# A chunk's two decays next to each other on ScalarE, and the query-score products moved up on VectorE

## The reference

```
decay = exp(where(incl, gc[..., :, None] - gc[..., None, :], -inf))
m     = where(strict, (k_beta @ k.T) * decay, 0)      # inverted: (I + m)^-1
intra = (q @ k.T) * decay                             # used for the outputs
```

## Time and profile before

| | |
|---|---|
| median of 3 runs | 1077.85 us (1075.97 to 1080.37) |
| the profiled execution | 1074.18 us, span 1072.4 us |
| mean granted TensorE clock | 0.935 of full |
| TensorE matmul busy | 907.4 us (85%) |
| VectorE busy | 652.2 us (61%) |
| ScalarE busy | 518.0 us (48%) |
| GpSimd busy | 187.0 us (17%) |

### The profile page before, as it was taken

How to read it: one execution, slowest core, us unless ns; L and a number is a source line. 1 busy time by engine, 2 the same in 40 slices (tenths; PEclk the granted TensorE clock), 3 DMA queues, 4 the chain that set the end, 5 groups by cost and what they waited for, 6 DMA issues and landing times. The chain is left out here.

```text
span 1072.4 us, 14130 instructions
## 1 busy us (share of the span) xinstructions
PE 907.4 (85%) x5500; PEld 768.4 (72%) x5500; DVE 652.2 (61%) x840; ACT 518.0 (48%) x827; POOL 187.0 (17%) x323
## 2 busy tenths in 40 slices
PE   3999888988889888898676998794799999999982
PEld 0578777887778777788675878774587877777761
DVE  1277455444665446644364544656888888888874
ACT  2365542325433354332562214434477777777761
POOL 3103050012500125001241000003212111111103
PEclk9899988999899998999987999895999999999996
DMA  8555546433474334743447342770689999999973
GB/s 302 178 174 152 131 100 198 123 94 92 95 222 119 94 99 89 215 124 94 165 127 212 120 129 93 252 273 2 217 315 368 389 388 378 381 374 385 382 303 138
DMA packets 218893, 216.79 MB, mean 202 GB/s; under 512 B 33168, under 2 KB 154681, under 8 KB 218185
## 3 DMA queue, kind: packets, MB, share of 16 engines
q1 hardware_dynamic: 216089, 205.90, 59.3%
q0 software_dynamic: 2736, 9.96, 2.4%
HBM read 194.83 MB, written 21.00 MB: 201 GB/s over the span
## 5 line engine op out<-in xcount | busy, mean ns | idle before, releaser
L1911 DVE TENSOR_TENSOR w_lo<-raw,w_hi 128x2048 fp32r<-128x2048 f32 x96 | 224.8, 2351 | 48.0 <-ACT w_hi L1383 47.4
L2114 PE MATMUL bank<-hT,half_hi 128*128 128x256 f32 (+1 forms) x1024 | 238.2, 329 | 16.1 <-ACT staged L1079 12.6
L1383 ACT CAST w_hi<-raw 128x2048 fp32r<-128x2048 f32 x96 | 183.3, 1911 | 79.7 <-DMA raw<-in_w_e_dram 68.1
L2114 PEld LDWEIGHTS bank<-hT,half_hi 128*128 128x128 f32 x1024 | 175.8, 201 | 33.2 <-ACT staged L1079 13.6
L1509 DVE TENSOR_TENSOR half_lo<-half_raw,half_hi 128x1024 fp32r<-128x1024 f32 x88 | 108.9, 1239 | 108.2 <-ACT half_hi L981 107.8
L2114 PE MATMUL bank<-hT,half_lo 128*128 128x256 f32 (+1 forms) x512 | 164.7, 322 | 0.0
L2114 PE MATMUL bank<-lane 128*128 128x128 f32 (+1 forms) x1072 | 140.9, 292 | 24.6 <-DMA lane<-inverse 13.3
L2114 PEld LDWEIGHTS bank<-lane 128*128 128x128 f32 (+1 forms) x1072 | 130.1, 199 | 35.5 <-issue 19.4
L2114 PE MATMUL bank<-w_hi,window 128*128 128x512 f32 x480 | 155.3, 399 | 0.0
L2114 PEld LDWEIGHTS bank<-hT,half_lo 128*128 128x128 f32 x512 | 102.7, 201 | 6.1
L981 ACT CAST half_hi<-half_raw 128x1024 fp32r<-128x1024 f32 x88 | 92.3, 1052 | 30.0 <-PE bank L2114 15.8
(11 more groups left out here) (302 smaller groups left out, 1312.5 us busy)
## 6 DMA issues: line engine op xcount, KB each, us to landing
raw<-in_w_e_dram SPq DMA_DIRECT2D x96, 1024.0 KB, 7.8
half_raw<-in_w_in_dram SPq DMA_DIRECT2D x64, 512.0 KB, 4.2
half_raw<-in_w_ada_dram SPq DMA_DIRECT2D x32, 512.0 KB, 4.2
raw<-in_w_ada_dram SPq DMA_DIRECT2D x8, 1024.0 KB, 9.8
expert_rows<-y_out POOLq DMA_DIRECT2D x15, 512.0 KB, 7.4
dense<-staged SPq DMA_DIRECT2D x32, 128.0 KB, 2.8
lane<-inverse SPq DMA_DIRECT2D x16, 256.0 KB, 5.5
lane<-inverse_turned SPq DMA_DIRECT2D x16, 256.0 KB, 5.3
```

The source lines that it names most:

```text
L1383: act.copy(e_hi[n % WBUF][:, :], raw[n % RING][:, :]).then_inc(s["hi_ready"], 1)
L1911: dve.tensor_tensor(e_lo[n % WBUF][:, :], raw[n % RING][:, :], e_hi[n % WBUF][:, :].bitcast(F32), ALU.subtract)\
L2114: return nc.tensor.matmul(dst, lhsT, rhs, start=start, stop=stop)
```

## The change

In the loop over pairs 0 to 2, ScalarE makes `intra_exp(2)` right behind `decay_exp(2)`, ahead of the rounding of a weight half and of `decay_exp(3)`, and `intra_exp(3)` right behind `decay_exp(3)`. Both stood later, `intra_exp(2)` between the output scaling of the pair before and `dense_copy`, `intra_exp(3)` between `center(1)` and `squares(0, 0)`. VectorE makes `intra_mask(2)` right behind `first_level(3)`, ahead of the low part of a weight half and of `taps(0)`; it stood between `taps(0)` and `silu(0)`. `intra_mask(3)` stays. No instruction and no wait is added or removed, TensorE's, SP's and GpSimd's orders are as they were, and pair 3 keeps its order.

```diff
@@ ScalarE, loop over pairs 0 to 2
                 ahead(CHAN_AT[j, 0])
                 decay_exp(1)
                 decay_exp(2)
+                intra_exp(2)
                 ahead(CHAN_AT[j, 1])
                 decay_exp(3)
+                intra_exp(3)
                 ahead(DENSE_AT[3 + 7 * i + 0])
                 center(0)
                 if i:
                     o_mul(i - 1)
-                intra_exp(2)
                 dense_copy(3 + 7 * i + 0)
                 tanh(0)
                 center(1)
-                intra_exp(3)
                 squares(0, 0)
                 ahead(DENSE_AT[3 + 7 * i + 1])
                 tanh(1)
@@ VectorE, loop over pairs 0 to 2
                 ahead(CHAN_AT[j, 1])
                 first_level(2)
                 first_level(3)
+                intra_mask(2)
                 ahead(DENSE_AT[3 + 7 * i + 0])
                 taps(0)
-                intra_mask(2)
                 silu(0)
                 taps(1)
                 intra_mask(3)
```

## The result

The changed kernel takes 1082.47 us (median of 20 runs, 1080.16 the lowest), the kernel before, in the 20 runs beside it, 1077.19. The ratio is 1.005 with a 95% interval of 1.003 to 1.0071: half a per cent slower. One run of the changed kernel, at 1206.97 us and a granted clock of 0.732, counts in its median (1082.20 without it) and not in the ratio.

A forecast was written before the change was run, and what follows sets the result against it. Bound: TensorE's wait for the scaled keys, set by a chain of ScalarE, VectorE, SP, DMA and GpSimd running beside it. 3 pairs x 1.4 = +4.2 us on the median 1077.85 gave 1082.0 us; range 1077 to 1087.

The forecast's parts named there:

- (a): ScalarE: early `intra_exp(2)` takes 1.70 us, delays the weight half's rounding by that, and fits the 1.78 us gap before `decay_exp(3)`.
- (b): VectorE: the half's low part (L1509) delays `first_level(2)` and the third tile's `m_ready` 1.7 us, `first_level(3)` only 0.3.
- (c): SP and DMA: rows of tiles 0 to 2 leave 1.7 us late, tile 3's 0.3; blocks 1.4 late per pair.
- only the last row move counts: Rival at the row moves: blocks only 0.3 us late per pair, +1.0 us, 1078.9 us; chance 0.18.
- (d): VectorE, first silu: late taps (0.6 us) and bare tanh (0.7) offset the moved product; silu 0.1 late, not 1.3 early.
- (e): TensorE, pairs 1 and 2: `turn_out` no longer waits for `intra_exp(3)`, so `turn_channels(0)` starts 1.9 us sooner; pair 0 unchanged.
- (f): TensorE before `turn_back(0, 0)`: the 1.9 us gain is lost waiting for keys; stalls become 4.0, 5.2 and 5.9 us.
- The clock: TensorE after the longer stall for the keys: extra time at the lower clock priced at 0, bounds 0 to 0.3 per pair.
- One to one to the end of the pair: Premise for everything behind `turn_back(0, 0)`: fixed order, so a shift there passes undiminished to the pair's end.
- a sign of being wrong: Later part of the pair (inverse loads, 3.16 us stall in pair 0): prediction fails if it takes up the lateness.
- The slower rival: At the blocks: full 1.7 us arrives plus 0.2 from queueing with the weight half; 5.7 us, 1083.6 us; chance 0.27.
- The faster rival: TensorE's 1.9 us gain in two pairs reaches the end: -3.8 to -7.5 us, 1074.1 to 1070.4; chance 0.08.

The follow-up runs named there:

- The second: Kernel before with only `intra_exp(2)` moved to right behind `decay_exp(2)`, `intra_exp(3)` and both products left in place: 1081.68 us, ratio 1.0046.
- the first experiment: Changed kernel with `intra_exp(2)` one place later, behind the rounding of the weight half, still ahead of `decay_exp(3)`: 1077.65 us, ratio 1.0012.
- sixth experiment: Changed kernel with SP issuing the load of a 512 KB weight half behind `move_blocks` instead of ahead of it: 1081.94 us, ratio 1.0051.
- ninth experiment: On top of the first experiment, `first_level(2)` on VectorE and the first row move on SP go ahead of the weight half: 1078.32 us, ratio 0.9998.
- third: Changed kernel with GpSimd's `key_norm(0)` made inside the block solve, ahead of its sixth step: 1070.18 us, ratio 0.9937; run again, 1071.21 us, 0.9951.
- fourth: Kernel before with GpSimd's `key_norm(0)` made inside the block solve, ahead of its sixth step: 1073.75 us, ratio 0.9967.
- eighth: Changed kernel with `intra_exp(2)` split, its four Relus ahead of the rounding of the weight half, its Exp behind it: 1079.43 us, ratio 1.0039.

## Why the prediction came out right

The forecast was 1082.0 us, 4.2 above the median before, and the slower side of half a per cent at 0.28. Measured are 1082.47 and 1.005, on the bound itself. Some of the closeness is luck. The kernel before came out 0.66 lower over 20 runs than over the three that the forecast stood on, so the forecast of 4.2 us missed by 0.8 to 1.2: the distance is 5.0 to 5.4 us, near the upper edge of the forecast's own band (1.8 per pair, 5.4). And the range had a slip that did not matter: its lower bounds, 0.9 above the median less 3 for the scatter, give 1075.8 and not 1077. Step by step:

(a) *The rounding 1.7 late, the fourth decay spared.* Held: 13.7 against 12.0 us, and 14.9 against 14.8.

(b) *VectorE passes it on.* Held: L1509 1.7 late, `first_level(2)` behind it. The second and the first experiment show that this one position makes and removes the loss.

(c) *Of the 1.7, 1.4 arrive at the blocks.* The mechanism held, the term was too small and one part of it wrong. First rows to fetch of the blocks is 6.5, 6.3 and 6.2 us before and 6.4, 7.75 and 6.5 after, 6.2 in all pairs of the sixth experiment: at most 0.3 of the 1.7 is made up. I had the rows of tile 3 leave 0.3 late. They go in two issues, the third and fourth of the four. The third did begin 0.3 late, but took 1.62 us where it took 0.36 before, and so the fourth began 1.55 late: in pair 1 the four issues end at 264.34, 20.5 us into the pair, before at 264.35, 19.0 into it. The third issue in the queue's timelines in pair 1, of the changed kernel and of the kernel before:

```profile
261.99 1.62 SPq L511 DMA_DIRECT2D problem_rows<-lane  x1
...
263.21 0.36 SPq L511 DMA_DIRECT2D problem_rows<-lane  x1
```

How long it takes goes with how soon it follows the first two, the large ones of 384 KB: 0.6 us behind the second it takes 1.33 to 1.92 us, 1.0 behind it 1.23 to 1.33, and 2.0 or more behind it 0.36, over all pairs of all runs here. In the first two cases it ends 2.4 to 3.0 us after the first issue began, whichever pair one takes. So the last, small move hangs on the first, large ones, and the rival "only the last row move counts" failed in its first sentence, the blocks 0.3 late: in no pair of the changed kernel are they less than 1.6 late. What the Trainium skill gives ("DMA: Bandwidth & Descriptors", Anatomy of one DMA), a fixed 2 us plus bytes over 436 GB/s, pointed the same way as that rival; here the measurement decides, 3.3 us for 128 KB and 4.8 in the changed kernel, medians of two. Only with the ninth experiment's order, where the large moves went out 4 us ahead, do the 128 KB land in 2.1 to 2.5 us, about the 2.3 of that formula.

(d) *The first silu neither early nor late.* Held: 24.3 against 24.2 in pair 1; the taps went out late and the tanh stood bare, as the two sides of that sum had it.

(e) *`turn_channels(0)` 1.9 sooner in pairs 1 and 2, not in pair 0.* Held in every pair: 25.0 against 26.9, and 25.0 in pair 0.

(f) *Swallowed.* Held, and seen from three sides: the first experiment has the gain and no loss and lies at the kernel before (1.0012); the second has the loss and no gain and lies at the changed kernel (1.0046); the third and fourth free the keys, and the order of the two kernels turns round, in their medians though not beyond their intervals. The forecast of the stalls was 4.0, 5.2 and 5.9 us; they are 4.55, 6.31 and 5.58.

*The clock* was priced at 0, with up to 0.3 a pair. That bound was too small. In pair 1 of the changed kernel, after the 6.31 us stall and after a 4.70 us stall for the inverses, the rows are:

```profile
288.90:293.60 4.70, 4.64 (x13) 3.87 (x14) 3.56 (x5) 2.32 (x4) 0.53 (x1) 0.50 0.47 136
...
313.60:317.60 4.00, 4.00 (x21) 4.00 (x22) 1.38 (x2) 0.00 (x0) 0.00 (x0) 0.57 1.14 298
```

The first stretch is all at half clock (0.50), where the same stretch had 0.64 behind a stall of 1.93 us: 0.14 x 4.7, some 0.7 us more lost. The second is `level_p(0)`, which in the kernel before followed a stall of 1.73 us at full clock:

```profile
310.00:314.00 4.00, 4.00 (x36) 4.00 (x37) 3.04 (x6) 0.00 (x0) 0.00 (x0) 1.00 1.17 293
```

That is another 1.7 us (0.43 x 4.0) in this pair of this execution. Pair 1 lost 6.7 us in all: 2.7 up to `turn_back(0, 0)`, 2.4 from there to `level_p(0)` (24.6 us, 22.2 before; the wait for the inverses is 3.0 longer) and 1.6 from there to the next pair. It is not a steady price: pair 0 of the kernel before also waited over 3 us there, and its 32 products took 6.53 us, those of this pair 5.44.

*One to one to the end of the pair.* This premise is the weak step. In pair 0 the change came 1.67 us late to `turn_back(0, 0)`, 1.2 late to `level_p(0)` and 0.1 late to the next pair: the later part took the lateness up, which the prediction had named as a sign of being wrong. In pair 2 it was 1.4, 1.9 and 3.0. From `level_p(0)` to the next pair TensorE idles 5.12 to 5.14 us in 37 of the 39 pairs of all runs, and yet the stretch takes from 68.7 to 72.0 us: the rest is the granted clock, in the third column from the right (PEclk). Pair 0 before and after, then pair 1 before and after:

```profile
173.92:245.39 71.47, 64.67 (x508) 59.48 (x509) 33.31 (x60) 20.14 (x48) 6.20 (x10) 0.96 0.37 104
...
173.51:243.88 70.37, 63.58 (x508) 58.38 (x509) 33.35 (x61) 20.17 (x48) 6.22 (x10) 0.98 0.37 107
...
310.00:378.73 68.73, 61.93 (x509) 56.75 (x509) 34.09 (x62) 20.15 (x48) 6.21 (x10) 1.00 0.40 110
...
313.60:383.97 70.37, 63.57 (x508) 58.38 (x509) 33.29 (x60) 20.17 (x48) 6.21 (x10) 0.98 0.38 106
```

Behind a stall of at most 1.73 us for the inverses, or none, it is 68.7 to 69.6 us (8 pairs), behind a longer one 70.1 to 72.0 (30 of 31 pairs), and among these the longer stall is often not the dearer. So a shift reaches the pair's end only with such steps of 1 to 3 us on top, either way. That three of them add up to about the measured loss holds for the mean over many executions; no single trace shows it. With 1.6 in place of 1.4 in (c) the sum is 4.8; what the clock and the wait for the inverses add on the mean of many executions, one profile can't tell. Measured are 5.0 (medians, without the run at 1206.97) to 5.4 (ratio).

The slower rival had the right size (5.7) for a wrong reason: the load that shares the queue was taken from beside the rows in the sixth experiment and the time stayed. The faster rival fell with the first.

## What to carry to other kernels

A small group put into an engine's idle gap delays what is queued directly behind it, even when the next instruction that one watches, here the fourth decay, is untouched; follow the neighbour it was put in front of, through every engine that handles it in order, down to the DMA queue. When a stall is removed, look for the next point where the same engine waits for another chain: what was won in front of it shows only after that wait is gone. And lateness can cost in full where the same earliness shows nothing, as in the eighth and ninth experiments here, so one experiment in each direction tells more than two in the same.

## What the runs showed of the hardware

SP's issue of a transfer is not of fixed length. The third issue of a row move took 0.36 us when it followed the two large ones by 2.0 us or more, 1.23 to 1.33 when it followed by 1.0, and 1.33 to 1.92 when it followed by 0.6. The rate of the DMA engines does not decide it: the issue of 0.36 us fell where they moved 344 GB/s, and the one of 1.62 us where they moved 296 in the mean. A chain that counts issues as free will put one that follows large transfers closely too early.

A stall of TensorE can cost twice, as wait and as clock, but its length alone doesn't tell the second price. Over the 4 us behind it the granted clock had a mean of 0.50 to 0.65 after every stall of 4.0 us and more in the loop. After shorter ones it was either: 1.00 after 3.39 us in the eighth experiment's pair 0, 0.67 after 3.40 us in pair 2 of the kernel before. And after the same 1.67 us at the start of a pair it was 1.00 in 17 cases of 26 and 0.57 to 0.64 in the other nine. A forecast can take such a price only as steps with a chance, not as a sum.
